# Where expert weights wait: a fixed split of eight weight buffers, 18 experts copied to bfloat16 ahead of time, output weights scaled earlier, and u2 written by SP

## The reference

```python
shift1, scale1, gate1, shift2, scale2, gate2 = split(silu(c) @ w_ada + b_ada, 6)
u = layer_norm(x) * (1 + scale1) + shift1
q, k, v, g, p = split(u @ w_in, [512, 1024, 1536, 2048])
ret_out  = silu(g) * group_norm(retention(rotary(q), rotary(k), v)) * ret_gn_w   # 4 heads, chunks of 128
pool_out = (trailing_mean(p, windows 2, 4, 8, 16) - p) @ w_pool * pool_scale
mix = concat(ret_out, pool_out) @ w_out
x = layer_norm(ALPHA * x + gate1 * mix, ln1_w, ln1_b)
u2 = layer_norm(x) * (1 + scale2) + shift2
# top-1 of 4 groups, then top-2 of its 8 experts, for each token:
y = sum over chosen experts e of gate_e * ((silu(u2 @ w1[e]) * (u2 @ w3[e])) @ w2[e])
x = layer_norm(ALPHA * x + gate2 * y, ln2_w, ln2_b)
```

## Time and profile before

| | us |
|---|---|
| median of 3 runs | 1031.4 |
| lowest and highest | 1013.66, 1042.17 |
| the profiled execution | 1010.89 |
| its span on the slowest core (core 1) | 1009.1 |
| span of the 8 cores | 981.3 to 1009.1 |

### The profile page before, as it was taken

How to read it: one execution, slowest core, us unless ns; L and a number is a source line. 1 busy time by engine, 2 the same in 40 slices (tenths; PEclk the granted TensorE clock), 3 DMA queues, 4 the chain that set the end, 5 groups by cost and what they waited for, 6 DMA issues and landing times.

```text
span 1009.1 us, 11200 instructions; the slowest of 8 cores (981.3 to 1009.1 us)
## 1 busy us (share of the span) xinstructions
PE 654.3 (65%) x4072; PEld 380.4 (38%) x4072; DVE 530.5 (53%) x1222; ACT 332.4 (33%) x561; POOL 351.6 (35%) x382
## 2 busy tenths in 40 slices
PE   0259987479896798988667687667666765760000
PEld 0215554245554455446556343333323332420000
DVE  0884575257366697789876242233223322333867
ACT  3245556234433243233312232323322321321211
POOL 1214332123131122233314465354445444326112
PEclk9979898779897898887556987879978978995555
DMA  9999989843646126696311179889899699668995
GB/s 174 224 196 182 150 141 158 137 82 66 144 75 136 48 68 136 114 231 116 63 20 29 36 195 173 238 186 194 197 221 239 123 242 251 128 173 242 276 289 240
DMA packets 50934, 159.79 MB, mean 158 GB/s; under 512 B 15802, under 2 KB 16314, under 8 KB 49216
## 3 DMA queue, kind: packets, MB, share of 16 engines
q0 software_dynamic: 38496, 108.27, 57.7%
q1 hardware_dynamic: 12384, 50.80, 14.8%
HBM read 305.75 MB, written 58.20 MB: 361 GB/s over the span
## 4 chain that ended last, share of the span: by engine, by line
DMA 36%; PE 35%; DVE 12%; ACT 6%; issue 5%; POOL 5%; another core or an unknown queue 0%; POOLq 0%; DVEq 0%
DMA M<-w 10%; PE pp L1120 9%; PE pp L599 6%; DMA M<-ytok 5%; DMA M<-w_in 5%; DMA M<-w,M 4%; DMA M<-w_ada 4%; DMA M<-x 4%; PE pp L640 3%; PE pp L1137 3%; PE pp L830 3%; POOL RC L559 2%; DMA u2d<-M 2%; PE pp L877 2%; PE pp L807 2%
## 5 line engine op out<-in xcount | busy, mean ns | idle before, releaser
L1120 PE MATMUL pp<-M 128*128 128x512 bf16 (+1 forms) x504 | 143.0, 439 | 56.5 <-DMA M<-w 42.0
L1142 DVE SCALAR_TENSOR_TENSOR M<-pp,M,G 128x1024 f32<-128x1024 f32 x63 | 80.4, 1283 | 112.2 <-DMA ytok<-M 56.6
L559 POOL TENSOR_TENSOR RC<-RC 128x1 f32<-128x1 f32 x64 | 55.2, 863 | 191.8 <-DVE RC L558 153.4
L599 PE MATMUL pp<-M 128*128 128x512 bf16 x384 | 101.5, 414 | 10.4 <-ACT M L570 7.3
L1120 PEld LDWEIGHTS pp<-M 128*128 128x128 bf16 x504 | 53.4, 109 | 126.8 <-issue 47.0
L1124 DVE TENSOR_TENSOR M<-pp,M 128x256 bf16<-128x256 f32 x63 | 26.7, 424 | 135.2 <-ACT M L1123 130.6
L1087 POOL DMA_INDIRECT M<-u2d,M x63 | 65.0, 1032 | 86.3 <-PE pp L1096 65.1
L1123 ACT ACTIVATE M<-pp 128x256 f32<-128x256 f32 x63 | 24.1, 384 | 206.3 <-PE pp L1120 182.6
L1144 POOL DMA_INDIRECT ytok<-M x63 | 63.8, 1012 | 58.0 <-DVE M L1142 45.0
L1137 PE MATMUL pp<-M 128*128 128x512 bf16 (+1 forms) x252 | 70.2, 407 | 21.1 <-ACT M L1133 14.3
L1098 ACT ACTIVATE M<-pp 128x1024 bf16<-128x1024 bf16 x63 | 64.1, 1021 | 44.1 <-PE pp L1096 33.3
(11 more groups left out here) (223 smaller groups left out, 1242.7 us busy)
## 6 DMA issues: line engine op xcount, KB each, us to landing
M<-w POOLq DMA_DIRECT2D x24, 1536.0 KB
M<-x SPq DMA_DIRECT2D x32, 512.0 KB, 9.9
M<-w_ada POOLq DMA_DIRECT2D x12, 1024.0 KB
wbf<-w POOLq DMA_DIRECT2D x8, 1536.0 KB
M<-wbf SPq DMA_DIRECT2D x8, 1536.0 KB, 14.8
M<-ytok SPq DMA_DIRECT2D x16, 512.0 KB, 16.4
M<-ytok POOLq DMA_DIRECT2D x16, 512.0 KB
out<-M SPq DMA_DIRECT2D x16, 512.0 KB, 14.0
```

What stands on the lines that cost most here:

```text
L559: P.op("pool", lambda e: e.tensor_tensor(out=rs, in0=rs, in1=negh[:, 0:1], op=ALU.pow), [key + "rs", "negh"], [key + "rs"], 0.65)
L599: pe([lambda e, kc=kc: e.matmul(pb(bank), lhsT=u[:, kc, is_], rhs=wsl[blk][:, kc, :], start=(kc == 0), stop=(kc == 7)) for kc in range(8)] ...
L1120: return e.matmul(pb(bk), lhsT=uTg[pr][:, k, :], rhs=w13[:, k, :], start=(k == 0), stop=(k == 7))
L1142: dve(lambda e: e.scalar_tensor_tensor(out=yst[yb], in0=pp(yp), scalar=gslot[:, col:col + 1], in1=gate_b, op0=ALU.mult, op1=ALU.mult), ks ...
```

## The change

- `_plan`: experts take buffers 0 to 5 in turn (`s % 6`) and spare units buffers 6 and 7 (`d % 2`), where before any unit took the buffer that came free first. The load is issued when that buffer is free.
- `STAGED` holds experts 6 to 23, 18 of them instead of 8. `STAGE_AT` issues 14 copies beside tiles 6 to 15 of the projections, four more follow `a5` of tiles 10 to 13. `mb` of a copy is 2.5 for the scheduler instead of 4.2. The copy's code is otherwise as before.
- `ADA_AT` moves the chunks of `w_ada` to tiles 1, 3, 4, 5, 6, 7, 8 and 9; their loads use four buffers instead of two.
- `w_out` is loaded after tile 8, its gate row computed at tile 10, and two of its slices are scaled at each of tiles 10 to 13.
- The matrix that takes the previous tile into the pooling keeps its 16 columns that aren't zero.
- `a5`: ACT casts `xq` to bfloat16 in `xqb` (two buffers, which also take what the squares write, in place of `junk`), and SP writes it to DRAM.

```diff
-STAGED = [7, 10, 13, 16, 19, 22, 25, 28]
+STAGED = list(range(6, 24))
+STAGE_AT = {6: 1, 7: 1, 9: 1, 10: 2, 11: 2, 12: 2, 13: 2, 14: 2, 15: 1}
+ADA_AT = {1: 4, 3: 5, 4: 6, 5: 7, 6: 8, 7: 9, 8: 10, 9: 11}
...
-    last = -1
-    for i, u in enumerate(queue):
-        k = i if i < NSLOT else min(range(NSLOT), key=lambda q: free_at[q])
-        last = max(last, free_at[k])
-        slot[u], at[u] = k, last
-        assert last < pos[u]
+    for u in queue:
+        k = u[1] % 6 if u[0] == "s" else 6 + u[1] % 2
+        slot[u], at[u] = k, free_at[k]
+        assert free_at[k] < pos[u]
...
+        def ada_slot(j):
+            return j if j < 4 else (4, 5, 2, 3)[j % 4]
...
-                    fns.append(lambda e, gs=gs, g=g: e.matmul(pb(4)[:, gs], lhsT=pq[:, gs], rhs=amat[:, 1, g, :], start=False, stop=True))
+                    fns.append(lambda e, gs=gs, g=g: e.matmul(pb(4)[:, g * 128:g * 128 + 16], lhsT=pq[:, gs], rhs=amatp[:, g, :], start=False, stop=True))
...
-                if t in (3, 5, 6, 8, 9, 11, 12, 14):
+                for _ in range(STAGE_AT.get(t, 0)):
                     stage_w([len(P.ops) - 1])
...
-                if t % 2 == 1 and t < 16:
-                    j = 4 + t // 2
-                    ada_chunk(j)
-                    if j + 2 < 12:
-                        ada_load(j + 2)
+                if t in ADA_AT:
+                    ada_chunk(ADA_AT[t])
+                    if ADA_AT[t] + 2 < 12:
+                        ada_load(ADA_AT[t] + 2)
+                if t == 8:
+                    P.dma("pool", lambda e: e.dma_start(out=wout.rearrange("p k d -> p (k d)"), in_=w_out, max_dma_last_dim=8192), writes=["wout"], mb=4.2)
+                if t == 10:
+                    gate_row(4, gate_b, "gate_b", 1.0)
+                if 10 <= t <= 13:
+                    scale_wout(2 * t - 20)
+                    scale_wout(2 * t - 19)
...
-            P.dma("pool", lambda e: e.dma_start(out=u2d[t * 128:(t + 1) * 128, :], in_=xq), reads=[kx], writes=["u2d%d" % t], mb=0.5)
+            act(lambda e: e.activation(out=xqb[i], in_=xq, func=AF.Copy), [kx], ["xqb%d" % i], 1.06)
+            P.dma("sp", lambda e: e.dma_start(out=u2d[t * 128:(t + 1) * 128, :], in_=xqb[i]), reads=["xqb%d" % i], writes=["u2d%d" % t], mb=0.25)
...
+        late_copies = {10: 1, 11: 1, 12: 1, 13: 1}
         for t in range(8, NT):
             a5(t)
+            for _ in range(late_copies.get(t, 0)):
+                stage_w([len(P.ops) - 1])
...
         for p in range(NU + 1):
+            if staged[0] < len(STAGED) and p > 0:
+                stage_w([len(P.ops) - 1])
```

More of the change, by code:

```diff
@@ L525, in ada_chunk @@
         def ada_chunk(j):
-            sl = j if j < 4 else 4 + j % 2
+            sl = ada_slot(j)
             bank = 6 + j % 2
@@ L722, in build_nc @@
         P.dma("sp", lambda e: e.dma_start(out=amat0, in_=c_amat[:, 0:512]), writes=["amat0"], mb=0.25, after=late)
-        P.dma("sp", lambda e: e.dma_start(out=amat.rearrange("p k g t -> p (k g t)"), in_=c_amat[:, 512:1536]), writes=["amat"], mb=0.5, after=late)
+        P.dma("sp", lambda e: e.dma_start(out=M[:, s_ + 6144:s_ + 6720], in_=c_amat[:, 512:1088]), writes=["amat"], mb=0.3, after=late)
         a1_block(0)
@@ L739, in stage_w @@
             staged[0] += 1
-            P.dma("pool", lambda e: e.dma_start(out=wbf[i * 128:(i + 1) * 128, :], in_=w123[u * 128:(u + 1) * 128, :]), writes=["wb%d" % u], mb=4.2, after=after)
+            P.dma("pool", lambda e: e.dma_start(out=wbf[i * 128:(i + 1) * 128, :], in_=w123[u * 128:(u + 1) * 128, :]), writes=["wb%d" % u], mb=2.5, after=after)
         for b in range(4):
@@ L779, in a5_head @@
         def a5_head():
-            P.dma("pool", lambda e: e.dma_start(out=wout.rearrange("p k d -> p (k d)"), in_=w_out), writes=["wout"], mb=4.2)
-            gate_row(4, gate_b, "gate_b", 1.0)
-            for k in range(8):
-                if k < 4:
-                    dve(lambda e, k=k: e.scalar_tensor_tensor(out=wout[:, k, :], in0=wout[:, k, :], scalar=gnc[:, k:k + 1], in1=gate_b, op0=ALU.mult, op1=ALU.mult),
-                        ["gate_b", "colsb"], ["wout%d" % k], 1.2)
-                else:
-                    dve(lambda e, k=k: e.tensor_tensor(out=wout[:, k, :], in0=wout[:, k, :], in1=gate_b, op=ALU.mult), ["gate_b"], ["wout%d" % k], 1.2)
             P.dma("sp", lambda e: e.dma_start(out=ln1w_b, in_=ln1w.partition_broadcast(128)), writes=["ln1w"], after=lastw)
```

24 lines of the change are left out of this document (16 added, 8 removed).

## The result

The changed kernel takes 1124.9 us (median of 4 runs, 1115.2 to 1132.9), the kernel before 1024.6 us in the same comparison: 1.106 times as long, interval 1.090 to 1.121. The forecast was 950 us, faster.

The account below looks back on a forecast made before the run. PE was taken to bound the projections, DVE nearly the layer-norm tiles, and waits for weight loads the expert units. Terms -40 + 0 + 3 - 15 - 6 - 5 - 6 + 2 = -67 gave 944 us; forecast 950, range 915 to 990.

Parts of the forecast that it names:

- The copies, +3 us: Ten more weight copies, beside projections and layer-norm tiles, fit in free DMA time at 8 us each: +3 us (0 to +15).
- the rule on HBM: At about 358 GB/s of HBM per core a copy would take 13 us, the ten 132 us instead of 80.
- Late copies, 0 (up to +10): Four copies beside the layer-norm tiles, 32 us of work against 49 free from 480 to 540 us: 0 (up to +10).
- The expert stage, -40 us: Units 10 to 41 fall from 5.73 to 4.5 us each: -40 us (bounds -54 and -17).
- The two-and-six split: Separate buffers for experts and spares in the expert stage: issue points five and four units ahead stay, so 0.
- two bounds: For the new expert unit step: 3.7 us, PE's burst, and 5.8 us, the pace from sixth to tenth unit.
- The last eight experts, 0 (-7 to +25): Experts 24 to 31, all loaded directly at the end, take about 115 us against 120 before: 0 (-7 to +25).
- Output weights, pooling, ada, u2, casts: -15 - 6 - 5 - 6 + 2 = -30: Earlier output weights -15, narrower pooling matrices -6, sooner ada loads -5, u2 writes by SP -6, ACT's casts +2 us.
- The slower one: Rival: staged loads don't overlap on SP's queue, 7.4 us per expert unit, +53 in place of -40, 1037 us; chance 0.05.
- Hand-overs at 5.2 us: Rival: PE, ACT, DVE and POOL hand over too slowly, expert units at 5.2 us, 967 us; chance 0.14.
- A wait in place of the one removed: Rival: in the expert stage gathers or scatters replace the wait for `M<-w`, units still 5.73 us, 984 us; chance 0.07.
- signs of a wrong forecast: Middle units over 5 us, the first gather waiting for late copies, or PE stalling at tile 10 to 13 for output weights.

Follow-up runs that it names:

- the order mended: The changed kernel with the size that the scheduler assumes for a spare unit's load set to 1.3 MB instead of 0.1: 1071.7 us, ratio 1.050.
- a block with fourteen direct experts behind it: The twelve-copy kernel with staged experts 6 to 17 instead of every second one from 7 to 29, and a spare's load counted 1.3 MB: 1036.1 us, ratio 1.018.
- the spread: The rest of the change on the old buffer choice and order costs, with twelve copies (every second expert, 7 to 29) in 4 KB pieces: 997.3 us, ratio 0.977.
- both losses taken away: The changed kernel with one copy instead of 18 and a spare unit's load counted 1.3 MB instead of 0.1 for the order: 953.6 and 958.8 us.

## Why the prediction was wrong

**The copies, +3 us.** This is the step that failed most. It priced ten more copies; from eight to eighteen the first unit moves from 519.2 to 623.7 us in the median of the cores, by 104 us (the first seven cost 5.6), and 17 copies cost 105 us in all. Three things were wrong in it. The price of 8 us was read off a copy alone; in a row of copies it is 14.0, and I had dismissed the 13 us of the rule on HBM because "neither number uses up the free time". Second, the free time: 162 us of DMA time were free as a mean over 210 to 540 us, but the copies lie where they are issued, and 303 to 383 us is full to 0.98. Third, "what could they delay": I looked for x tiles, and found them prefetched. What was delayed were the layer-norm row and the writes of u2, short transfers that pay a piece of 32 KB for each of their own. The wait within a pair, which I did not see in the code, was no cost of its own in pieces of 32 KB: without it 1139.4 us.

**Late copies, 0 (up to +10).** Wrong: 40.6 us at the first unit. The 49 us free of the earlier trace rows were there, but a write of u2 took 36.2 us beside the late copies; ACT waited 24.1 us for it, and DVE and PE for ACT.

**The expert stage, -40 us.** The price of a unit was right, for another order: 4.6 us where I had 4.5, in the run with the order mended. In the changed kernel it was 6.4. The failed step stands at the opening of that part: "The two-and-six split alone therefore moves nothing; I cost it at 0, and its cover is that same lead." The split moves nothing, as its undoing showed; but the lead that I took is that of the plan, in units of the program's text. PE's stream is written by the scheduler, and there one unit stood between, where the text has two. The spare's load takes 6 to 7 us to land though it moves nothing; two units of PE's work hid it, one did not. The 4.5 itself was chosen between two bounds, so that 4.6 came is partly luck. Of each group of six I called 12 us a wait for a load, where the row has 6.27; and taking PE's waits for loads out of the kernel before (42.0 us to 2.8) brought it nothing in the median, since the waits for ACT took their place.

**The last eight experts, 0 (-7 to +25).** Behind the block a unit took 6.0 us with the order mended, before 5.5 (159 us for 232 matmuls), 13 us over 23 units; a block with fourteen direct experts behind it cost about 30 us against the spread. That is inside the range, but the mechanism was another: I priced direct loads one after another, and in both runs PE waits there for ACT's copies (26.8 us in 21 waits from 830 to 969 us with the order mended) and for no load. In the changed kernel as it is both exist, and PE does wait for `M<-w` and `M<-w,M` at the end, 33.8 us from 860 to 1000 us.

**Output weights, pooling, ada, u2, casts: -15 - 6 - 5 - 6 + 2 = -30.** About two thirds of it came: with the same eight copies the first unit is 20.7 us sooner in the median of the cores and the ratio 0.981 (0.974 to 0.989), some 20 us. (With one copy it is 26, but seven copies fewer are in that.) They were not taken apart, so no single one of the five terms is shown. A write of u2 stayed in the chain even with eight copies (12.7 us) and with one (15.7).

**What was to show it.** PE's wait for `M<-w` is gone in the middle and back at the end (16.2 us in 8 waits), the DMA share is lower in the middle (0.56) and above 0.9 at the end (0.97). SP's loads landed in 6.6 us, sooner than the 10 to 15. The steps of 4.5 us, PE busy after 303 us and a chain without u2 did not come. Of the signs of a wrong forecast, middle units over 5 us came (6.4); PE did not wait at tiles 10 to 13 for the output weights.

**The rivals.** None was it. The slower one, staged loads that don't overlap, is refuted: they land in 6.6 us. Hand-overs at 5.2 us are refuted for the order mended, where the middle units took 4.6, though hand-overs do pace the units behind a block. A wait in place of the one removed I had only as "gathers or scatters", at 0.07 and with the old pace as its worst; it was the spare's own load, and it costs more than the wait that it replaced. That 0.05 for slower was far too sure: both errors stood on means (free DMA time, lead of units) where a single late transfer decides.

**With both losses taken away** the kernel takes 954 to 959 us, against a forecast of 950 and a range of 915 to 990. So the two terms that I had at +3 and at 0 carry nearly all of the error; that the rest meets the forecast so closely is partly luck, since that run makes seven copies fewer than the kernel before and the smaller terms weren't measured one by one.

## What to carry to other kernels

A prefetch hides only as long as the engine's own stream leaves work between the event that frees the buffer and the one that needs the data: count it in the stream that the scheduler wrote, for the shortest case, and not in the plan. More lead is not better by itself: the orders with 2 or 3 units in between had no wait for loads and a new one for a shared PSUM bank. A copy from DRAM to DRAM should be priced by the bytes that it reads and those that it writes together, at the price under load: halving what was read (and dropping the change of type) took it from 14.0 us to 8.0; and whatever short transfer shares the engines can pay one of its long pieces for each of its own. Work that is moved into a stage's "free" time should be priced at its place, by what is waited for there.

## What was not expected of the hardware

- A copy of 3.1 MB read and 1.6 MB written takes 8 us of all engines alone and 14.0 us in a row of others; with half the bytes read and no change of type 8.0 us in a row.
- A write of 256 KB took 36.2 us beside copies in pieces of 32 KB, most of it seven turns of 4.8 us, where the median of the 16 such writes in the same execution is 3.7 us.
- A gather whose rows are all out of range still needs 6 to 7 us to land at a DMA share of 0.56, and over 14 us at a share of 0.97, where experts' direct loads stand ahead of it on the same queue.

```profile
901.96 15.85 DMA M<-w,M
...
954.45 14.66 DMA M<-w,M
```

- With no wait for loads PE's granted clock is 0.98 over 139 us of units; where PE waits for a load at every second unit, for up to 7.0 us, it is 0.80 over 194 us.
